# Attention values of two heads in one bank, with denominators from ScalarE's sums

## The chip, the cores and the metric

One NeuronCore of a Trainium2 chip runs the whole kernel. The metric is the device time in microseconds of one execution. Times inside the kernel come from one profiled execution, counted from the start of its span.

## The reference, cut to what matters

Two layers (DEPTH = 2) of a bidirectional encoder over 512 positions of width 1024, in float32. Each layer projects its normalised input, runs three mixers side by side (a Hyena convolution on 256 channels, grouped-query attention with 8 query heads and 2 key/value heads of 64, and multi-head latent attention, MLA, with 4 heads of 96 for scores and 64 for values), normalises each mixer's output, projects back, and then runs a gated feed-forward block of width 2816. The change is inside the two attentions:

```
s = einsum('bkgqd,bskd->bkgqs', qi, k) * scale
p = softmax(s, axis=-1)
o = einsum('bkgqs,bskd->bkgqd', p, v)
```

and the same for the four MLA heads, with a latent query and key of 64 + 32 and values of 64.

## The kernel before, in words

Every engine has its own program, in an order written out by hand, and the engines meet only at named semaphores. There is no planner: what stands behind a waiting instruction on its engine waits with it.

Activations are kept transposed (channels on partitions, the 512 positions along the free dimension). In the attention stage the twelve heads of a layer (h = 0 to 7 grouped-query, GH = 8; h = 8 to 11 MLA) pass one after another through a software pipeline. For a head TensorE does this:

- `scores(h)`: for each of four query chunks qc a bank 0 to 3 gets 128 queries by 512 keys. A grouped-query head uses two fp32r matmuls per chunk, on the rounded query with its low half (`q2`) below it; an MLA head one fp32 matmul, which runs as two passes. Chunk qc overwrites a bank that the exponentials of the head before must have read (`p_ready`), and grouped-query scores wait for `q2hi` and `q2lo` of their head.
- `turn(h, (0, 1))` and `turn(h, (2, 3))`: sixteen 128x128 transposes of the probabilities into banks 4 (even key chunk sc) and 5 (odd). A chunk waits until the one before it in the bank is copied out.
- `values(h)`: four fp32 matmuls (eight passes) into bank 6. The stationary tile has 128 columns: 64 of values and 64 of ones (the ones stand in `vg` and `mv`, set by two memsets of VectorE, lines 1438 and 1541). So 64 partitions of the bank get the output and the other 64 the denominator, repeated.
- `bank7(k)`: a piece of the MLA projections, two pieces per head for the first eight heads, in the order of the list `B7`: for each MLA head a query piece (6 passes), a rotation piece (a permutation, 2 passes) and a key piece (3 passes), then four value pieces. Bank 7 must be emptied by VectorE (`b7_free`) before the next one.
- `group(g)`: the sum of squares of a mixer's output.

TensorE's order (line 1161 on) is scores(h+1), the first bank-7 piece, turn(h, (0, 1)), values(h-1), turn(h, (2, 3)), the second bank-7 piece.

VectorE finds the maxima of a head's scores (`maxima`, which write `nm` and, scaled, `ns`), copies the odd turned chunks (`pt_copy`), does its part of the bank-7 pieces (for a rotation two products and a sum) and multiplies the output by the inverse denominator (`head_out`, line 1576). Its order is maxima(h+1), pt_copy(h, 1), bank-7 piece, head_out(h-1), pt_copy(h, 3), bank-7 piece.

ScalarE takes the exponentials (`exps`, four of 128x512), copies the even turned chunks, rounds the queries of head h+2 (`q_hi`, line 583) and forms the inverse denominators as Exp(-Ln(d)) on 64 partitions (`denominators`, line 714). Its order is pt_copy(h, 0), exps(h+1), q_hi(h+2), denominators(h-1), pt_copy(h, 2). The normalisation of the mixers (`group_squares`, `group_root`, `group_hi`) is put in at the last heads. GpSimd makes the low half of the rounded queries (`q_lo`, line 428).

Of the kernel before, what the change touches and what calls it, by code (L numbers as in the profile page):

```python
# [39 lines left out]
P = 128  # L40
DM, T, DEPTH = 1024, 512, 2
DC = DM // P
TC = T // P
# [62 lines left out]
def build(nc, a, out):  # L106
    ctx = ExitStack()
    with ctx:
# [29 lines left out]
        nm = sb("nm", [P, 2, TC])  # L138
        ns = sb("ns", [P, 2, TC])


# [83 lines left out]
        for name in (  # L225

                "ident_in", "fconst_in", "fw2_in", "const_in", "x_in0", "x_in1", "x_in2", "x_in3", "par_in", "w3_in",
                "filt_in", "tab_in", "mla_in", "raw0", "raw1", "out_sem",

                "raw_ok", "const_ok", "x_tr", "x_first", "fst_tr", "par_tr", "par_ok", "f_mm", "f_arg", "f_sin",  # L230

                "hi_ready", "lo_ready", "pe_item",

                "x_new", "gh_ready", "gl_ready", "xsq", "xsq_used", "xstat", "rbc_ready",

                "ysq", "ysq_used", "ycopy", "stat_post", "rms_post", "t_ready",

                "evac", "conv1", "conv_done", "nsq", "nstat", "nstd", "nrm", "nperm", "roped", "vtr", "vcopy", "khi", "klo",

                "fc_mm", "fc_done", "fd_mm", "fd_copy", "fd_done",  # L240

                "ha_mm", "hu_copy", "he_mm", "ho_mm", "he_copy", "h_prod", "hc_mm", "h_done",

                "q2hi", "q2lo", "s_tile", "nmax", "p_ready", "pt_tile", "pt_act", "pt_dve", "pv", "head_inv", "y_head",

                "mhi", "mlo", "kr_copy", "b7_full", "b7_free",

                "gsq", "gsq_used", "gstat", "gstd", "y_norm", "ygh", "ygl",

                "f_evac", "f_conv1", "f_conv", "f_gelu", "f_prod", "f_hi", "f_lo",  # L250

                "o_tr", "o_copy", "dve_self", "act_self"):
            S[name] = sem(name)
# [22 lines left out]
        assert len(B7) == 2 * GH  # L276
        HEADS = GH + MH


# [179 lines left out]
        def _(act):  # L459
# [83 lines left out]
            for lay in range(DEPTH):  # L543
# [127 lines left out]
                def group_root(g):  # L671

                    act.wait_ge(S["gstat"], lay * 3 + g + 1)

                    act.wait_ge(S["head_inv"], lay * HEADS + (GH, GH + 1, HEADS)[g])
# [20 lines left out]
                def exps(h):  # L696
                    scale = GD ** -0.5 if h < GH else MD ** -0.5
                    act.wait_ge(S["nmax"], lay * HEADS + h + 1)
                    if h >= 2:

                        act.wait_ge(S["pt_tile"], lay * 4 * HEADS + 4 * (h - 1))
                    for qc in range(TC):
                        A(prob[:, h % 2, qc, :], ps[:, qc, :], ACT.Exp, bias=ns[:, h % 2, qc:qc + 1],  # L703
                          scale=scale).then_inc(S["p_ready"], 1)

                def pt_copy(h, sc):

                    act.wait_ge(S["pt_tile"], lay * 4 * HEADS + 4 * h + sc + 1)
                    if h >= 2 and sc == 0:

                        act.wait_ge(S["pv"], lay * HEADS + h - 1)
                    A(probT[h % 2][:, sc, :], ps[:, 4, :], ACT.Copy).then_inc(S["pt_act"], 1)

                def denominators(h):

                    act.wait_ge(S["pv"], lay * HEADS + h + 1)
                    swapped = (h // 4) % 2 if h < GH else h % 2
                    o_rows = slice(GD, 2 * GD) if swapped else slice(0, GD)
                    d_rows = slice(0, GD) if swapped else slice(GD, 2 * GD)

                    if h >= 2:
                        act.wait_ge(S["y_head"], lay * HEADS + h - 1)
                    inverse_root(rr[o_rows, h % 2, :], std[o_rows, :], ps[d_rows, 6, :], 1,
                                 bias=False).then_inc(S["head_inv"], 1)

                exps(0)
                for h in range(HEADS):
                    pt_copy(h, 0)
                    if h + 1 < HEADS:
                        exps(h + 1)  # L730
                    if h + 2 < GH:
                        q_hi(h + 2)
                    if h:
                        denominators(h - 1)
                    pt_copy(h, 2)
                    if h == 1:
                        kr_copies()
                    if h == GH - 1:
                        group_squares(0)
                    if h == GH:  # L740
                        group_root(0)
                        act.wait_ge(S["y_head"], lay * HEADS + GH)
                        group_squares(1)
                    if h == GH + 1:
                        group_root(1)
                    if h == GH + 2:
                        group_hi(0)
                    if h == GH + 3:
                        group_hi(1)
                denominators(HEADS - 1)  # L750
                act.wait_ge(S["y_head"], lay * HEADS + HEADS)
                group_squares(2)
# [63 lines left out]
        def _(pe):  # L816
# [87 lines left out]
            for lay in range(DEPTH):  # L904
# [224 lines left out]
                def turn(h, tiles_):  # L1129

                    pe.wait_ge(S["p_ready"], (lay * HEADS + h) * 4 + 4)
                    for sc in tiles_:
                        if sc >= 2 or h:

                            k = (lay * HEADS + h) * 2 + sc // 2
                            pe.wait_ge(S["pt_act" if sc % 2 == 0 else "pt_dve"], k)
                        for qc in range(TC):
# [4 lines left out]
                def values(h):  # L1142

                    if h:
                        pe.wait_ge(S["y_head"], lay * HEADS + h)
                    if h == 0:
                        pe.wait_ge(S["vcopy"], lay + 1)
                    if h == GH:
                        pe.wait_ge(S["b7_free"], lay * len(B7) + len(B7))
                    pe.wait_ge(S["pt_act"], (lay * HEADS + h) * 2 + 2)  # L1150
                    pe.wait_ge(S["pt_dve"], (lay * HEADS + h) * 2 + 2)
                    for sc in range(TC):
                        if h < GH:
                            v = vg[:, sc, (h // 4) * GD:(h // 4) * GD + P]
                        else:
                            i = h - GH
                            v = mv[:, sc, i // 2, (i % 2) * MV:(i % 2) * MV + P]
# [17 lines left out]
                values(HEADS - 1)  # L1175

# [15 lines left out]

                pe.wait_ge(S["y_head"], lay * HEADS + HEADS)
                pe.wait_ge(S["gstd"], lay * 3 + 3)
# [48 lines left out]
        def _(dve):  # L1243
# [60 lines left out]
            for lay in range(DEPTH):  # L1304
# [235 lines left out]

                V.do(nc.vector.memset(mv[:, :, :, MV:2 * MV], 1.0))
                def maxima(h):
# [7 lines left out]
                def pt_copy(h, sc):  # L1550

                    dve.wait_ge(S["pt_tile"], (lay * HEADS + h) * 4 + sc + 1)
                    if h >= 2 and sc == 1:

                        dve.wait_ge(S["pv"], lay * HEADS + h - 1)
                    copy(probT[h % 2][:, sc, :], ps[:, 5, :]).then_inc(S["pt_dve"], 1)
# [18 lines left out]

                def head_out(h):

                    swapped = (h // 4) % 2 if h < GH else h % 2
                    o_rows = slice(GD, 2 * GD) if swapped else slice(0, GD)
                    rows = slice((h % 2) * GD, (h % 2 + 1) * GD)  # L1580
                    dst = qf[rows, h // 2, :] if h < GH else cq[rows, (h - GH) // 2, :]
                    if h < GH:

                        dve.wait_ge(S["q2lo"], lay * GH + h + 1)
                    dve.wait_ge(S["head_inv"], lay * HEADS + h + 1)
                    tt(dst, ps[o_rows, 6, :], rr[o_rows, h % 2, :], ALU.mult).then_inc(S["y_head"], 1)

# [4 lines left out]
                for h in range(HEADS):  # L1592
# [5 lines left out]
                    if h == GH + 3:  # L1598
                        dve.wait_ge(S["y_head"], lay * HEADS + GH)
                        group_norm(1)  # L1600
                    if h:
                        head_out(h - 1)
                    pt_copy(h, 3)
# [8 lines left out]
                    if h == GH + 3:  # L1612
                        group_lo(0)
                        group_lo(1)
                head_out(HEADS - 1)
                dve.wait_ge(S["y_head"], lay * HEADS + HEADS)
                group_sum(2)
# [141 lines left out]
```

## Time and profile before

| | us |
|---|---|
| median of 3 runs | 1548.88 (1548.32 to 1549.81) |
| profiled execution, its own time | 1550.24 |
| its span in the profile | 1548.2 |
| TensorE matmuls busy | 1428.5 (92%) |
| VectorE busy | 923.2 (60%) |
| ScalarE busy | 612.1 (40%) |
| GpSimd busy | 521.2 (34%) |

The profile calls the engines PE (TensorE matmuls), PEld (its weight loads), DVE (VectorE), ACT (ScalarE) and POOL (GpSimd). L1158 is line 1158 of the kernel. A matmul's end is modelled, so how long a matmul occupies the engine is read from the start of the next one. A granted clock of 1.00 is 2.4 GHz, half of it 1.2 GHz. "[2.08 <-POOL q L433]" behind an instruction says that its engine sat idle for 2.08 us before it and that GpSimd's instruction of line 433 ended this. The attention stage of layer 0 lies between about 205 and 330 us, that of layer 1 between about 963 and 1088 us.

### The profile page before, as it was taken

To read this page: it belongs to the slowest core of one execution; us is meant where nothing else is said; L and a number is where in the kernel's file an instruction comes from. 1 tells how busy PE (TensorE), PEld (TensorE's weight loads), DVE (VectorE), ACT (ScalarE), POOL (GpSimd) and SP (SyncE) were. 2 spreads that over 40 slices of the span, in tenths; PEclk is the share of its full clock that TensorE was granted. 3 is DMA by queue.
4 is the path that set the end of the run, shared out by engine and by line. 5 is a ranking of instruction groups with operands and counts; after the bars stand their busy time and mean duration, and the time that the engine had idled before them with its cause. 6 is when DMAs were issued, how large, how long until landed. Compare 5 with 4: busy or idle time off the path is not lost.

```text
span 1548.2 us, 14920 instructions
## 1 busy us (share of the span) xinstructions
PE 1428.5 (92%) x5759; PEld 1056.5 (68%) x5759; DVE 923.2 (60%) x1033; ACT 612.1 (40%) x867; POOL 521.2 (34%) x243
## 2 busy tenths in 40 slices
PE   5898989988899999999978898999979999999997
PEld 3576746556688888878755775664757888887885
DVE  5636777564678787711166567666465878785112
ACT  5222255653444444332241224556344444433222
POOL 2312211014444444444441213100354444444444
PEclk8999999999899999999989999999989999999998
DMA  7211100002133333323241112000112333332231
GB/s 241 74 28 54 48 28 1 1 28 82 41 96 95 95 96 95 92 85 97 80 136 41 55 31 72 1 1 1 55 55 82 96 96 95 95 95 89 86 102 64
DMA packets 195167, 108.52 MB, mean 70 GB/s; under 512 B 5895, under 2 KB 193657, under 8 KB 194202
## 3 DMA queue, kind: packets, MB, share of 16 engines
q1 hardware_dynamic: 195098, 107.58, 23.5%
q8 instruction: 46, 0.75, 0.2%
q14 instruction: 23, 0.19, 0.0%
HBM read 105.47 MB, written 2.10 MB: 69 GB/s over the span
## 4 chain that ended last, share of the span: by engine, by line
PE 75%; DVE 11%; ACT 6%; issue 3%; POOL 3%; DMA 1%; POOLq 0%; SPq 0%; DVEq 0%; ACTq 0%
PE ps L877 19%; PE ps L879 19%; PE ps L878 19%; PE ps L1158 3%; PE ps L984 2%; PE ps L945 2%; DVE nm L1546 2%; PE ps L971 2%; ACT prob L703 2%; POOL xT L416 2%; POOL wl L409 1%; PE ps L887 1%; ACT rr L479 1%; PE ps L1138 1%; ACT wh L468 1%
## 5 line engine op out<-in xcount | busy, mean ns | idle before, releaser
L409 POOL TENSOR_TENSOR wl<-raw,wh 128x1024 fp32r<-128x1024 f32 x184 | 443.5, 2412 | 895.6 <-ACT wh L468 895.6
L468 ACT ACTIVATE wh<-raw 128x1024 fp32r<-128x1024 f32 x184 | 194.9, 1060 | 613.4 <-PE ps L879 608.7
L877 PE MATMUL ps<-gh,wh 128*128 128x512 f32 (+1 forms) x896 | 365.2, 408 | 11.2 <-POOL wl L409 11.2
L879 PE MATMUL ps<-gh,wl 128*128 128x512 f32 (+1 forms) x896 | 355.7, 397 | 0.0
L878 PE MATMUL ps<-gl,wh 128*128 128x512 f32 (+1 forms) x896 | 355.5, 397 | 0.0
L877 PEld LDWEIGHTS ps<-gh,wh 128*128 128x128 f32 (+1 forms) x896 | 167.6, 187 | 58.6 <-issue 12.6
L878 PEld LDWEIGHTS ps<-gl,wh 128*128 128x128 f32 (+1 forms) x896 | 167.7, 187 | 45.8 <-issue 4.7
L879 PEld LDWEIGHTS ps<-gh,wl 128*128 128x128 f32 (+1 forms) x896 | 167.7, 187 | 42.8
L1651 DVE SCALAR_TENSOR_TENSOR cv<-pad,pm,cv 128x512 f32<-128x512 f32 x88 | 130.6, 1484 | 84.0 <-ACT cv L779 84.0
L1260 DVE TENSOR_TENSOR acc<-acc,sq 128x512 f32<-128x512 f32 x24 | 60.6, 2523 | 195.9 <-ACT sq L508 195.7
L877 PE MATMUL ps<-fh,wh 128*128 128x512 f32 x352 | 139.3, 396 | 3.2 <-POOL wl L409 3.2
L878 PE MATMUL ps<-fl,wh 128*128 128x512 f32 x352 | 139.0, 395 | 0.0
L879 PE MATMUL ps<-fh,wl 128*128 128x512 f32 x352 | 139.0, 395 | 0.0
L1638 DVE TENSOR_TENSOR fl<-fprod,fh 128x512 fp32r<-128x512 f32 x44 | 103.9, 2362 | 15.2 <-ACT fh L792 15.2
L877 PEld LDWEIGHTS ps<-fh,wh 128*128 128x128 f32 x352 | 66.0, 187 | 20.2 <-ACT wh L468 4.0
L879 PEld LDWEIGHTS ps<-fh,wl 128*128 128x128 f32 x352 | 66.0, 187 | 16.2
L878 PEld LDWEIGHTS ps<-fl,wh 128*128 128x128 f32 x352 | 66.0, 187 | 16.0
L779 ACT ACTIVATE cv<-pad,pm 128x512 f32<-128x512 f32 x88 | 70.5, 803 | 0.0
L1654 DVE SCALAR_TENSOR_TENSOR cv<-pad,pm,cv 128x512 f32<-128x512 f32 x88 | 66.2, 752 | 3.1
L1646 DVE TENSOR_TENSOR pad<-ps,rbc 128x512 f32<-128x512 f32 x88 | 56.4, 684 | 18.9 <-ACT rbc L479 18.9
L703 ACT ACTIVATE prob<-ps,ns 128x512 f32<-128x512 f32 x96 | 58.1, 690 | 18.3 <-DVE ns L1548 18.1
L1138 PEld LDWEIGHTS ps<-ident,prob 128*128 128x128 f32 x384 | 44.5, 141 | 25.1 <-issue 19.8
(224 smaller groups left out, 1950.2 us busy)
## 6 DMA issues: line engine op xcount, KB each, us to landing
raw<-w_up SPq DMA_DIRECT2D x88, 512.0 KB, 3.8
raw<-w_down SPq DMA_DIRECT2D x32, 512.0 KB, 3.6
raw<-w_in SPq DMA_DIRECT2D x30, 512.0 KB, 3.9
raw<-w_out SPq DMA_DIRECT2D x16, 512.0 KB, 3.6
raw<-w_down SPq DMA_DIRECT2D x16, 384.0 KB, 3.2
xio<-x SPq DMA_DIRECT2D x4, 512.0 KB, 5.7
win<-c_win SPq DMA_DIRECT2D x2, 1024.0 KB, 5.5
TF<-c_tf SPq DMA_DIRECT2D x2, 1024.0 KB, 10.0
```

The lines of the kernel that those rows point to most:

```text
L409: nc.gpsimd.tensor_tensor(wl[:, slot, :], raw[:, slot, :], wh[:, slot, :].bitcast(F32), ALU.subtract).then_inc(S["lo_ready"], 1)
L468: A(wh[:, slot, :], raw[:, slot, :], ACT.Copy).then_inc(S["hi_ready"], 1)
L703: A(prob[:, h % 2, qc, :], ps[:, qc, :], ACT.Exp, bias=ns[:, h % 2, qc:qc + 1], scale=scale).then_inc(S["p_ready"], 1)
L779: A(cv[:, k, :], pad[:, k, 1:T + 1], ACT.Identity, scale=pm[:, bass.ds(col + j + (PM["ffn_w1"] + k * FC), 1)], bias=pm[:, bass.ds(col + j ...
L877: mm(ps[0:cols, bank, :], w_hi, x_hi, start=start and k == 0, stop=False)
L878: mm(ps[0:cols, bank, :], w_hi, x_lo, start=False, stop=False)
L879: ins = mm(ps[0:cols, bank, :], w_lo, x_hi, start=False, stop=stop and k == tile_n - 1)
L1138: ins = nc.tensor.transpose(ps[:, 4 + sc % 2, qc * P:(qc + 1) * P], prob[:, h % 2, qc, sc * P:(sc + 1) * P], ident[:])
L1260: tt(acc[:], acc[:], sq[:, m % 2, :], ALU.add).then_inc(S["ysq_used"], 1)
L1638: tt(fl[:, j:j + 1, :], fprod[:].rearrange("p (o t) -> p o t", o=1), fh[:, j:j + 1, :].bitcast(F32), ALU.subtract).then_inc(S["f_lo"], 1)
L1651: V.do(stt(out=c, in0=pad[:, k, 0:T], scalar=pm[:, bass.ds(col + j + (PM["ffn_w0"] + k * FC), 1)], in1=c, op0=ALU.mult, op1=ALU.add))
L1654: stt(out=c, in0=pad[:, k, 2:T + 2], scalar=pm[:, bass.ds(col + j + (PM["ffn_w2"] + k * FC), 1)], in1=c, op0=ALU.mult, op1=ALU.add).then_i ...
```

## The change

Heads are taken in six pairs (PAIRS = HEADS // 2).

- `values(p)` of TensorE now does both heads of a pair: for each of four key chunks, one matmul of 64 value columns for the even head into partitions 0 to 63 of bank 6 and one for the odd head into partitions 64 to 127. The ones and their memsets are gone.
- It no longer stands between the two turn pairs of each head. It stands, with a new `inverses(p)`, before the first turns of each even head from 2 on, and at the end.
- The exponentials also sum their row (`accum_out`) into `den`. VectorE takes the reciprocal for a pair (`denominators(p)`, in odd heads), ScalarE spreads it over 64 columns per head (`inv_wide`, into `std`), TensorE turns that in four transposes into bank 4 (`inverses`), and ScalarE copies it to `rr` (`inv_copy`).
- ScalarE's Ln and Exp of the denominators are gone. The output is multiplied once per pair on 128 partitions (`pair_out`).
- The exponentials of head h (from 2 on) wait for the reciprocal of the pair before; the turns of an even head wait for `inv_copy`.
- The roots and high halves of mixer groups 0 and 1 on ScalarE move by up to one head, and wait for `inv_tile`, since they share `std`.

```diff
 exps(h), ScalarE
+                    if h >= 2:
+                        act.wait_ge(S["den_inv"], lay * PAIRS + h // 2)
...
                         A(prob[:, h % 2, qc, :], ps[:, qc, :], ACT.Exp, bias=ns[:, h % 2, qc:qc + 1],
-                          scale=scale).then_inc(S["p_ready"], 1)
+                          scale=scale, accum_out=den[:, h % 2, qc:qc + 1]).then_inc(S["p_ready"], 1)
...
+                def inv_wide(p):
+                    act.wait_ge(S["den_inv"], lay * PAIRS + p + 1)
+                    if p:
+                        act.wait_ge(S["inv_tile"], lay * PAIRS + p)
+                    A(std[:].rearrange("p (c h d) -> p h c d", c=TC, h=2), inv[:].unsqueeze(3).to_broadcast([P, 2, TC, GD]),
+                      ACT.Copy).then_inc(S["inv_wide"], 1)
+                def inv_copy(p):
+                    act.wait_ge(S["inv_tile"], lay * PAIRS + p + 1)
+                    if p >= 2:
+                        act.wait_ge(S["y_pair"], lay * PAIRS + p - 1)
+                    A(rr[:, p % 2, :], ps[:, 4, :], ACT.Copy).then_inc(S["inv_copy"], 1)
                 exps(0)
                 for h in range(HEADS):
+                    if h and h % 2 == 0:
+                        inv_copy(h // 2 - 1)
                     pt_copy(h, 0)
                     if h + 1 < HEADS:
                         exps(h + 1)
                     if h + 2 < GH:
                         q_hi(h + 2)
-                    if h:
-                        denominators(h - 1)
                     pt_copy(h, 2)
+                    if h % 2:
+                        inv_wide(h // 2)
...
 TensorE
+                def inverses(p):
+                    pe.wait_ge(S["inv_wide"], lay * PAIRS + p + 1)
+                    pe.wait_ge(S["pt_act"], (lay * HEADS + 2 * p + 1) * 2 + 2)
+                    for qc in range(TC):
+                        at = slice(qc * P, (qc + 1) * P)
+                        ins = nc.tensor.transpose(ps[:, 4, at], std[:, at], ident[:])
+                    ins.then_inc(S["inv_tile"], 1)
...
                     for sc in range(TC):
-                        if h < GH:
-                            v = vg[:, sc, (h // 4) * GD:(h // 4) * GD + P]
...
-                        ins = mm(ps[:, 6, :], v, probT[h % 2][:, sc, :], start=(sc == 0), stop=(sc == TC - 1))
+                        for half in range(2):
+                            if p < GH // 2:
+                                at = 2 * GD * (p // 2)
+                                v = vg[:, sc, at:at + GD]
+                            else:
+                                v = mv[:, sc, p - GH // 2, 2 * MV * half:2 * MV * half + MV]
+                            ins = mm(ps[half * GD:(half + 1) * GD, 6, :], v, probT[half][:, sc, :], start=(sc == 0), stop=(sc == TC - 1))
...
                         bank7(2 * h)
+                    if h and h % 2 == 0:
+                        inverses(h // 2 - 1)
+                        values(h // 2 - 1)
                     turn(h, (0, 1))
-                    if h:
-                        values(h - 1)
                     turn(h, (2, 3))
...
 VectorE
-                V.do(nc.vector.memset(vg[:, :, GD:2 * GD], 1.0))
-                V.do(nc.vector.memset(mv[:, :, :, MV:2 * MV], 1.0))
+                def denominators(p):
+                    dve.wait_ge(S["p_ready"], (lay * HEADS + 2 * p + 1) * 4 + 4)
+                    if p:
+                        dve.wait_ge(S["inv_wide"], lay * PAIRS + p)
+                    nc.vector.reciprocal(inv[:], den[:]).then_inc(S["den_inv"], 1)
+                def pair_out(p):
+                    dst = qf[:, p, :] if p < GH // 2 else cq[:, p - GH // 2, :]
...
+                    tt(dst, ps[:, 6, :], rr[:, p % 2, :], ALU.mult).then_inc(S["y_pair"], 1)
...
-                    if h:
-                        head_out(h - 1)
+                    if h % 2:
+                        denominators(h // 2)
+                    elif h:
+                        pair_out(h // 2 - 1)
                     pt_copy(h, 3)
```

## Rows read from the trace of the kernel before

**Rows 1.** The page, part 4: the chain of work that ended last, by engine

```profile
PE 75%; DVE 11%; ACT 6%; issue 3%; POOL 3%; DMA 1%; POOLq 0%; SPq 0%; DVEq 0%; ACTq 0%
```

**Rows 2.** Stretches: length, busy (xcount) PE, PEld, DVE, ACT, POOL; clock, DMA

```profile
224.46:290.50 66.04, 64.62 (x271) 40.01 (x269) 42.63 (x79) 39.81 (x67) 6.38 (x5) 1.00 0.00 1
290.50:327.40 36.90, 33.23 (x126) 17.93 (x124) 24.87 (x43) 24.97 (x42) 0.00 (x0) 1.00 0.00 1
991.58:1057.60 66.02, 64.60 (x264) 39.11 (x263) 42.52 (x80) 39.69 (x67) 5.10 (x4) 1.00 0.00 0
```

**Rows 3.** Timeline of head 1: start, length, engine, line, what [idle before <-releaser]

```profile
224.46 1.04 PE L1138 MATMUL ps<-ident,prob 128*128 128x128 f32 x8
...
225.10 0.60 ACT L712 ACTIVATE probT<-ps 128x512 f32<-128x512 f32 x1 [5.88 <-PE ps L1138]
...
225.34 3.60 PE L1158 MATMUL ps<-probT,vg 128*128 128x512 f32 x8
225.54 0.69 DVE L1556 COPY probT<-ps 128x512 f32<-128x512 f32 x1 [0.89 <-PE ps L1138]
225.59 2.42 ACT L703 ACTIVATE prob<-ps,ns 128x512 f32<-128x512 f32 x4
...
228.03 0.63 ACT L588 ACTIVATE q<-qf 64x512 fp32r<-64x512 f32 x1
...
228.81 1.27 POOL L433 TENSOR_TENSOR q<-qf,q 64x512 fp32r<-64x512 f32 x1 [8.66 <-ACT q L588]
...
229.56 0.47 PE L1116 MATMUL ps<-cqh,uqh 128*96 128x512 f32 x1
...
231.03 0.39 PE L1093 MATMUL ps<-ka,q 128*128 128x512 f32 x1
...
232.84 1.02 PE L1119 MATMUL ps<-mqf,perm_m 96*96 96x512 f32 x2
...
233.71 1.04 PE L1138 MATMUL ps<-ident,prob 128*128 128x128 f32 x8
```

**Rows 4.** Groups of 225 to 290: line, engine, shapes, xcount | busy, mean ns

```profile
L1122 PE MATMUL ps<-ckl,ukh 128*64 128x512 f32 x3 | 1.2, 394 | 0.0
```

**Rows 5.** Timeline of head 0

```profile
214.70 1.03 PE L1138 MATMUL ps<-ident,prob 128*128 128x128 f32 x8
...
216.07 1.10 PE L1138 MATMUL ps<-ident,prob 128*128 128x128 f32 x8 [0.34 <-ACT probT L712]
...
217.11 1.10 PE L1119 MATMUL ps<-mqf,perm_m 96*96 96x512 f32 x2
...
220.29 0.47 PE L1093 MATMUL ps<-ka,q 128*128 128x512 f32 x1 [2.08 <-POOL q L433]
...
223.51 0.63 PE L1122 MATMUL ps<-ckh,ukh 128*64 128x512 f32 x1
```

**Rows 6.** Timeline of head 5, VectorE: its copy and its part of the rotation

```profile
263.77 0.69 DVE L1556 COPY probT<-ps 128x512 f32<-128x512 f32 x1
...
265.69 0.69 DVE L1568 TENSOR_TENSOR mqf<-yt 96x512 f32<-96x512 f32 x1
```

**Rows 7.** Chain of waits, window of layer 0's attention: start, length, what

```profile
270.64 0.69 PE ps L1126 x3
...
277.21 3.44 PE ps L1100 x8
```

**Rows 8.** Timeline of the last four heads

```profile
306.57 3.60 PE L1100 MATMUL ps<-mkf,mqf 96*128 96x512 f32 x8
...
324.29 3.67 PE L1158 MATMUL ps<-probT,mv 128*128 128x512 f32 x8 [1.88 <-DVE probT L1556]
```

**Rows 9.** Timeline ahead of head 0

```profile
205.80 0.48 DVE L1541 MEMSET mv<- 128x512 f32 x1 [0.17 <-DVE ckv L1397]
```

**Rows 10.** Groups of the whole span, ScalarE

```profile
L533 ACT ACTIVATE pm<-ps 128x88 f32<-128x88 f32 (+1 forms) x6 | 1.2, 240 | 3.3 <-PE ps L847 3.3
```

More of the change, by code:

```diff
@@ L139, in build @@
         ns = sb("ns", [P, 2, TC])
+        den = sb("den", [P, 2, TC])
+        inv = sb("inv", [P, 2, TC])
         with ExitStack() as s:
@@ L277, in build @@
         HEADS = GH + MH
+        PAIRS = HEADS // 2
         @block.sync
@@ L709, in pt_copy @@
                     if h >= 2 and sc == 0:
-                        act.wait_ge(S["pv"], lay * HEADS + h - 1)
+                        act.wait_ge(S["pv"], lay * PAIRS + h // 2)
                     A(probT[h % 2][:, sc, :], ps[:, 4, :], ACT.Copy).then_inc(S["pt_act"], 1)
[L714 to L724, printed above, removed]
+                def inv_wide(p):
[9 more added lines that the diff above has]
+                    A(rr[:, p % 2, :], ps[:, 4, :], ACT.Copy).then_inc(S["inv_copy"], 1)
                 exps(0)
                 for h in range(HEADS):
+                    if h and h % 2 == 0:
+                        inv_copy(h // 2 - 1)
                     pt_copy(h, 0)
@@ L740, in _ @@
                     if h == GH:
+                        act.wait_ge(S["inv_tile"], lay * PAIRS + GH // 2)
                         group_root(0)
-                        act.wait_ge(S["y_head"], lay * HEADS + GH)
+                        act.wait_ge(S["y_pair"], lay * PAIRS + GH // 2)
                         group_squares(1)
-                    if h == GH + 1:
+                    if h == GH + 2:
+                        act.wait_ge(S["inv_tile"], lay * PAIRS + GH // 2 + 1)
                         group_root(1)
-                    if h == GH + 2:
                         group_hi(0)
@@ L749, in _ @@
                         group_hi(1)
-                denominators(HEADS - 1)
-                act.wait_ge(S["y_head"], lay * HEADS + HEADS)
+                inv_copy(PAIRS - 1)
+                act.wait_ge(S["y_pair"], lay * PAIRS + PAIRS)
                 group_squares(2)
@@ L1136, in turn @@
                             pe.wait_ge(S["pt_act" if sc % 2 == 0 else "pt_dve"], k)
+                        if h and h % 2 == 0 and sc == 0:
+                            pe.wait_ge(S["inv_copy"], lay * PAIRS + h // 2)
                         for qc in range(TC):
@@ L1174, in _ @@
                         group(h - GH)
-                values(HEADS - 1)
+                inverses(PAIRS - 1)
+                values(PAIRS - 1)
                 def gate_out(k):
@@ L1191, in _ @@
                     tiles(lay, I_OUT + m, m, m, DC, yh, yl, 0, True, True, gate=gate_out, ks=range(ready, DC))
-                pe.wait_ge(S["y_head"], lay * HEADS + HEADS)
+                pe.wait_ge(S["y_pair"], lay * PAIRS + PAIRS)
                 pe.wait_ge(S["gstd"], lay * 3 + 3)
@@ L1553, in pt_copy @@
                     if h >= 2 and sc == 1:
-                        dve.wait_ge(S["pv"], lay * HEADS + h - 1)
+                        dve.wait_ge(S["pv"], lay * PAIRS + h // 2)
                     copy(probT[h % 2][:, sc, :], ps[:, 5, :]).then_inc(S["pt_dve"], 1)
@@ L1574, in bank7 @@
                         copy(mv[:, i, :, 2 * MV:3 * MV], v[:, :, 1, MN:MN + MV]).then_inc(S["b7_free"], 1)
[L1576 to L1586, printed above, removed]
+                def denominators(p):
+                    dve.wait_ge(S["p_ready"], (lay * HEADS + 2 * p + 1) * 4 + 4)
+                    if p:
+                        dve.wait_ge(S["inv_wide"], lay * PAIRS + p)
+                    nc.vector.reciprocal(inv[:], den[:]).then_inc(S["den_inv"], 1)
+                def pair_out(p):
+                    dst = qf[:, p, :] if p < GH // 2 else cq[:, p - GH // 2, :]
+                    if p < GH // 2:
+                        dve.wait_ge(S["q2lo"], lay * GH + 2 * p + 2)
+                    dve.wait_ge(S["pv"], lay * PAIRS + p + 1)
+                    dve.wait_ge(S["inv_copy"], lay * PAIRS + p + 1)
+                    tt(dst, ps[:, 6, :], rr[:, p % 2, :], ALU.mult).then_inc(S["y_pair"], 1)
                 maxima(0)
@@ L1614, in _ @@
                         group_lo(1)
-                head_out(HEADS - 1)
-                dve.wait_ge(S["y_head"], lay * HEADS + HEADS)
+                pair_out(PAIRS - 1)
+                dve.wait_ge(S["y_pair"], lay * PAIRS + PAIRS)
                 group_sum(2)
```

21 lines of the change are left out of this document (8 added, 13 removed).

## The prediction

> **What bounds the kernel now.** I read three views. The chain that ended last gives TensorE 75% of the span [rows 1]. The stretches show what its attention stage is like: from head 1's first turn to head 8's it takes 66.04 us with TensorE busy for 64.62 at full clock, and layer 1 repeats it to 0.02 us; the last four heads, to the end of the last values, take 36.90 us with 33.23 busy [rows 2]. So the stage is TensorE's, with almost nothing left over in the first part. The timeline of one head shows why [rows 3]: after the turns of score chunks 0 and 1 begin (224.46) a chain runs elsewhere. ScalarE copies chunk 0 at 225.10, takes head 2's four exponentials from 225.59, and rounds head 3's queries at 228.03; GpSimd makes their low half from 228.81 to 230.08. Only then may TensorE start head 3's scores. It never notices: values(0) stand in that place from 225.34, eight passes of 0.43 us, 3.43 in all, then two more turns and a piece for bank 7 (229.56), and the scores start at 231.03, 0.95 us after they could. The change touches just this place.
>
> **What the change does to the work.** Below, a is the start of a head's turns of chunks 0 and 1, and V the time of one pair's values.
>
> *Values.* Before: 8 passes a head. After: 16 passes for two heads, each of 64 stationary columns. A pass of 64 columns streams the same 512 and costs the same (394 ns modelled, as the 96-column ones around it) [rows 4], so there is no gain unless the two halves of the array work at once. Bounds: 16 passes in a row, 6.86 us a pair as now; all of them in twos, 3.43 us. I take V = 4.3, ten pass times. No row shows two halves in use, so this is a judgement: the diff alternates the halves after every matmul, and they share no stationary column, no moving tile and no output partition. The turn for both ends goes into the range.
> The Trainium skill, "TensorE: Matmul & The Clock Gate", Part 3 (packing small matmuls), says that matmuls whose outputs start in different column groups run concurrently, and gives 2.38 times for three tiles; at that efficiency (0.79 of ideal) an estimate for two is 6.86/1.59 = 4.3 us. Against the change, "TensorEngine Tiling (Array Packing)", Key Properties, says that changing the tiling mode drains the array, and each pair now does so twice. No row here shows either.
>
> *Inverses.* Four turns of 128 columns a pair: the eight of head 1 take 0.88 us (224.46 to 225.34), so 0.44, 12 times. They need ScalarE's wide copy, which lies behind the second copy of the odd head and ends at about a + 7, ahead of the next scores' end (below): no wait. ScalarE's copy back (0.6) fits into V. The reciprocal (VectorE, 128x8) costs at most what the smallest row there costs, some 0.2.
>
> *The move.* This is the expensive part. values() leaves its place between a head's two turn pairs and goes ahead of the first, for even heads only. Now the two turn pairs follow each other, and the chain ScalarE copy, exponentials, query copy, GpSimd, next scores has only 2.4 us of turns and one bank-7 piece over it. How long the chain is can be read where no values stand in between even now, at head 0 [rows 5]: turns at 214.70, second turns 216.07 (they wait for the copy out of bank 4), next piece 217.11, and head 2's scores at 220.29 after 2.08 us idle for GpSimd. That is a + 5.59. It holds for every head 0 to 5 afterwards. In head 1 the same sum gives 230.08 + 0.15 - 224.46 = 5.77; I use 5.6.
>
> *The new wait.* Exponentials of an even head overwrite den, so they wait for the reciprocal, which VectorE takes in the odd head before only after its copy of chunk 1 (ends a + 1.77) and a bank-7 piece. A copy of 0.68 makes that a + 2.5 instead of a + 1.13: +1.4 us on the chain in heads 1 and 3. In head 5 the piece is the rotation, which ends 2.61 us after the copy begins [rows 6], so at a + 3.7, and exponentials at a + 3.9: +2.8. Queued behind it on ScalarE are the query copy and the second copy; behind these GpSimd and the scores.
>
> *The walk.* Scores 1.81 (231.03 to 232.84), rotation piece 0.87, query piece 1.47, key or value piece 0.69, MLA scores 3.43 [rows 3, 7]. Time from one head's turns to the next one's:
> head 1: 5.6 + 1.4 + 1.81 + 0.87 + 0.44 + V = 10.12 + V
> head 2: 5.6 + 1.81 + 1.47 = 8.88
> head 3: 5.6 + 1.4 + 1.81 + 0.69 + 0.44 + V = 9.94 + V
> head 4: 5.6 + 1.81 + 0.87 = 8.28
> head 5: 5.6 + 2.8 + 1.81 + 0.69 + 0.44 + V = 11.34 + V
> Heads 6 and 7 feed MLA scores, which need no query copy and wait only for the first exponential: 3.2 + 3.43 + 0.69 = 7.32 and 3.2 + 3.43 + 0.44 + V = 7.07 + V.
> Sum 62.95 + 4V; with V = 4.3 it is 80.1 against 66.04: +14.1 us a layer, although the passes themselves got 10 us shorter.
> Last four heads: after head 8's turns ScalarE does copy, exponentials, copy (a + 4.3), root (1.35), four squares; VectorE's sums end at a + 9.1, its maxima of head 10 at 11.75, copy and reciprocal at 12.65, so head 11's scores start at 13.85 (now 306.57 - 290.50 = 16.07 [rows 8]). Then 3.43 + 0.44 + V to head 10's turns, and from there 10.2 (exponentials, root and the high halves on ScalarE, the norm and reciprocal on VectorE, wide copy, inverses) + V to the end: 27.9 + 2V = 36.5 against 36.90, -0.4.
>
> *Clock.* In head 0 TensorE passed from full to half clock in that 2.08 us gap, in both layers: the scores behind it took 220.29 to 223.51, 3.22 us instead of 1.81, with 0.2 more in the piece after [rows 5]. An idle of 1.88 us at 324.29 left the clock up [rows 8]. The gaps of the walk run from the end of the bank-7 piece (which starts at 2.5 when VectorE has emptied the bank, 3.95 where it rotates first) to the next scores: 7.0 - 3.97 = 3.0, 7.0 - 3.4 = 3.6 and 8.4 - 4.65 = 3.7 us in heads 1, 3 and 5, 5.6 - 4.65 = 0.9 and 5.6 - 3.97 = 1.6 in heads 2 and 4. I count three falls of 1.6 us a layer: +4.8 (bounds 0 and 5 x 1.6 = 8).
>
> *Rest.* The memset of mv lay ahead of the first maxima [rows 9]: -0.4. Sums beside the exponentials: no row has such an operation. Bounds: nothing, and one small ScalarE instruction each, 0.24 us [rows 10]. I take 0.1 each, 4 on the chain in some 6 heads: +2.4 (0 to 5.8). Ln and Exp of the denominators (1.22 us a head) leave ScalarE, and VectorE multiplies 128 partitions once for two heads: neither was late, so nothing. What follows the last values (norm of group 2) has 8 us of output passes over it, as before.
>
> *Sum.* A layer: 14.1 - 0.4 + 4.8 + 2.4 - 0.4 = +20.5; two: +41. The profiled execution took 1550.24 us (span 1548.2), so 1591.2; the median of the runs is 1.4 lower: **1590 us**.
>
> **The rivals.**
> *The halves do not overlap.* V = 6.86: the walk gives 90.4 (+24.4) and the last four 41.6 (+4.7), with the other terms +35.9 a layer, +72: 1621. For it: every pass in the trace starts 0.43 us after the one before, whatever its columns. Against it: none of these passes went to another part of the array.
> *TensorE stays the bound.* If the chain were covered, each layer would save 6 x (6.86 - 4.3) - 6 x 0.44 = 12.7 us, two 25: 1523, faster. Its place is the start of scores(h+2). It decides from where the chain ends before a + 3.4 to 4.0, when turns and bank-7 piece are done; it would have to be 2 us shorter than head 0 shows it. For it only TensorE's 98% busy; against it the order of the instructions.
> *No difference.* The overlap's gain (15.4 a layer) and a chain seen in part only just cancel: 1549. This needs half of the stalls to be absent; nothing speaks for it.
> *The clock stays down.* If all of heads 1 to 7 ran at half clock, scores (5 x 1.81 + 2 x 3.43), pieces (about 6) and values (17) would take as long again: +39 a layer in place of 4.8, 1658. For it: TensorE would be busy for some 70% of that stretch; against it: after head 0 the clock was up again at the end of one head's scores.
>
> **How the numbers follow.** Forecast 0.58, no overlap 0.27, TensorE the bound 0.07, no difference 0.03, clock down 0.05. Within the forecast the ends are 1565 (V = 3.43, no fall of the clock, free sums) and about 1610; no overlap reaches to 1628 with dear sums. The range 1568 to 1628 leaves out the fast cases, the clock and little else. A measurement of this kernel tells 0.2%, 3 us, from no change. Slower by more: 0.90; within: 0.03; faster: 0.07.
>
> **What would show it.** Scores of heads 2 to 7 preceded by idle time of TensorE, ended by GpSimd, of 3 us or more behind odd heads and 1 to 1.6 behind even ones; turn pairs back to back with 0.5 us for the copy; exponentials of even heads starting after the reciprocal; granted clock under 1 in the stretch of heads 1 to 7; 16 passes of values in some 4.3 us (starts under 0.43 apart) or in 6.9. Wrong, if these scores start without a wait, if that stretch is under 66 us, or if the wait is ended by something other than GpSimd's low half.

## The result

The changed kernel takes 1604.7 us (median, 1601.82 to 1605.62) against 1549.35 us for the kernel before on the same chip (median of 1548.32, 1548.88, 1549.81 and one stray execution of 3313.44 us, which the interval leaves out); ratio 1.036, 95% interval 1.034 to 1.038. The forecast was 1590 us in a range of 1568 to 1628. Way and cause were right. Two terms, the clock and the last four heads, were too small, and V was too large, so that the errors partly cancelled.

The page after gives TensorE slightly more busy time, and its chain of waits more TensorE, ScalarE and GpSimd than [rows 1]:

```profile
PE 1432.1 (90%) x5807; PEld 1055.9 (66%) x5807; DVE 921.4 (58%) x1029; ACT 602.5 (38%) x939; POOL 521.3 (33%) x243
```
```profile
PE 77%; DVE 9%; ACT 7%; POOL 4%; issue 4%; DMA 1%; POOLq 0%; SPq 0%; DVEq 0%; ACTq 0%
PE ps L892 18%; PE ps L890 18%; PE ps L891 18%; PE ps L1184 3%; ACT prob L708 3%; PE ps L997 2%; PE ps L958 2%; PE ps L984 2%; PE ps L1106 2%; PE ps L1154 2%; POOL xT L419 1%; PE ps L1113 1%; PE ps L1107 1%; POOL wl L412 1%; PE ps L900 1%
```

Busy time is a little longer although the passes of values now overlap, because passes at the lower clock take longer. The line that has grown most is the first half of the grouped-query scores: 64 instructions, behind 43.2 us of idle time, 35.4 of them ended by GpSimd's low half of the queries.

```profile
L1106 PE MATMUL ps<-ka,q 128*128 128x512 f32 x64 | 39.1, 612 | 43.2 <-POOL q L436 35.4
```

Stretches of layer 0 from head 1's first turns to head 8's, and from there to the first output pass (columns as in [rows 2]: length, busy time of PE, PEld, DVE, ACT, POOL, granted clock, DMA):

```profile
224.35:314.75 90.40, 70.24 (x294) 41.69 (x292) 44.92 (x84) 38.10 (x89) 6.30 (x5) 0.85 0.00 1
314.75:355.68 40.93, 31.80 (x127) 16.86 (x125) 22.29 (x38) 22.63 (x50) 0.00 (x0) 0.79 0.00 1
```

66.04 us have become 90.40, 36.90 have become 40.93, and the granted clock is 0.85 and 0.79 where it was 1.00 [rows 2]. In layer 1 the same two stretches take 89.45 and 38.55 us at clock 0.87:

```profile
1009.55:1099.00 89.45, 69.30 (x294) 40.95 (x292) 44.71 (x84) 38.09 (x89) 6.30 (x5) 0.87 0.00 0
1099.00:1137.55 38.55, 29.41 (x127) 15.65 (x125) 22.43 (x38) 22.58 (x50) 0.00 (x0) 0.87 0.00 1
```

Before they took 66.01 (982.34 to 1048.35) and 36.89 (to 1085.24). Together that is 28.4 us more in layer 0 and 25.1 in layer 1, 53.5 in all; the profiled spans differ by 51.8 (1600.0 against 1548.2), so the rest of the kernel is 1.7 us shorter.

Head 1 in the timeline answers to [rows 3]; there the scores of head 3 began 6.57 us after the turns (224.46 to 231.03) with values inside, here 7.54 after, with none:

```profile
224.35 1.03 PE L1154 MATMUL ps<-ident,prob 128*128 128x128 f32 x8
...
224.99 0.60 ACT L717 ACTIVATE probT<-ps 128x512 f32<-128x512 f32 x1 [5.89 <-PE ps L1154]
...
225.73 1.10 PE L1154 MATMUL ps<-ident,prob 128*128 128x128 f32 x8 [0.34 <-ACT probT L717]
...
226.63 0.18 DVE L1607 RECIPROCAL inv<-den 128x8 f32<-128x8 f32 x1
...
226.90 0.69 ACT L708 ACTIVATE prob<-ps,ns 128x512 f32<-128x512 f32 x1 [1.31 <-PE ps L1154]
...
227.49 0.19 ACT L708 ACTIVATION_READ_ACCUMULATOR prob<-ps,ns 128x1 f32 x1
...
227.58 0.68 ACT L708 ACTIVATE prob<-ps,ns 128x512 f32<-128x512 f32 x1
...
229.71 0.63 ACT L591 ACTIVATE q<-qf 64x512 fp32r<-64x512 f32 x1
...
230.48 1.26 POOL L436 TENSOR_TENSOR q<-qf,q 64x512 fp32r<-64x512 f32 x1 [10.47 <-ACT q L591]
230.98 0.63 ACT L725 ACTIVATE std<-inv 128x512 f32<-128x512 f32 x1
...
231.89 0.77 PE L1106 MATMUL ps<-ka,q 128*128 128x512 f32 x1 [3.50 <-POOL q L436]
...
235.44 1.91 PE L1132 MATMUL ps<-mqf,perm_m 96*96 96x512 f32 x2
...
237.14 0.75 PE L1164 MATMUL ps<-ident,std 128*128 128x128 f32 x4
...
237.82 3.65 PE L1184 MATMUL ps<-probT,vg 128*64 128x512 f32 x16
...
241.41 0.77 PE L1154 MATMUL ps<-ident,prob 128*128 128x128 f32 x5
```

The reader sees: the second turns at a + 1.38, after the copy; the reciprocal at 226.63 and the exponentials right behind it (226.90); the sum's read (0.19) behind each, so that four exponentials take 2.8 us instead of 2.4; the query copy at 229.71, GpSimd at 230.48, the scores at 231.89. Scores and rotation then last 5.25 us at half clock (to 237.14) where they took 2.68 before. And the 16 passes of values take 3.59 us (237.82 to 241.41). The scores of heads 4 to 7 wait in the same way:

```profile
247.56 0.66 PE L1106 MATMUL ps<-ka,q 128*128 128x512 f32 x1 [1.46 <-POOL q L436]
...
260.09 0.77 PE L1106 MATMUL ps<-ka,q 128*128 128x512 f32 x1 [4.15 <-POOL q L436]
...
274.98 0.76 PE L1106 MATMUL ps<-ka,q 128*128 128x512 f32 x1 [1.91 <-POOL q L436]
...
288.20 0.77 PE L1106 MATMUL ps<-ka,q 128*128 128x512 f32 x1 [4.22 <-POOL q L436]
```

Two more gaps of 1.26 us lie ahead of the bank-7 pieces that wait for VectorE's rotation (245.20 and 283.08).

### The profile page after: what moved, and what is told of

Read it like the earlier page. It is cut to its first block, busy times and chain, and to the rows that moved or that the text cites. A ratio compares the mean times of both kernels' runs of the same rounds, so it can differ in the third digit from the quotient of the medians.

```text
span 1600.0 us, 15092 instructions
## 1 busy us (share of the span) xinstructions
PE 1432.1 (90%) x5807; PEld 1055.9 (66%) x5807; DVE 921.4 (58%) x1029; ACT 602.5 (38%) x939; POOL 521.3 (33%) x243
## 4 chain that ended last, share of the span: by engine, by line
PE 77%; DVE 9%; ACT 7%; POOL 4%; issue 4%; DMA 1%; POOLq 0%; SPq 0%; DVEq 0%; ACTq 0%
PE ps L892 18%; PE ps L890 18%; PE ps L891 18%; PE ps L1184 3%; ACT prob L708 3%; PE ps L997 2%; PE ps L958 2%; PE ps L984 2%; PE ps L1106 2%; PE ps L1154 2%; POOL xT L419 1%; PE ps L1113 1%; PE ps L1107 1%; POOL wl L412 1%; PE ps L900 1%
## 5 line engine op out<-in xcount | busy, mean ns | idle before, releaser
L1684 DVE SCALAR_TENSOR_TENSOR cv<-pad,pm,cv 128x512 f32<-128x512 f32 x88 | 130.7, 1485 | 83.5 <-ACT cv L792 83.5
L1572 DVE TENSOR_REDUCE nm<-ps 128x1 f32<-128x512 f32 x96 | 63.8, 688 | 47.0 <-PE ps L1107 38.0
L1106 PE MATMUL ps<-ka,q 128*128 128x512 f32 x64 | 39.1, 612 | 43.2 <-POOL q L436 35.4
L1154 PE MATMUL ps<-ident,prob 128*128 128x128 f32 x384 | 55.7, 290 | 22.0 <-ACT probT L717 16.2
L708 ACT ACTIVATE prob<-ps,ns 128x512 f32<-128x512 f32 x96 | 64.6, 689 | 24.9 <-DVE ns L1574 11.8
```

The lines of the kernel that those rows point to most:

```text
L1106: mm(ps[:, qc, :], q2[:, h % 2, cols], ka[:, h // 4, :], start=True, stop=False)
L1572: V.do(nc.vector.reduce_max(nm[:, h % 2, qc:qc + 1], ps[:, qc, :], AX.X))
L1684: V.do(stt(out=c, in0=pad[:, k, 0:T], scalar=pm[:, bass.ds(col + j + (PM["ffn_w0"] + k * FC), 1)], in1=c, op0=ALU.mult, op1=ALU.add))
```

## The experiments

All times are medians, each beside runs of the kernel before on the same chip (1548.8 to 1549.1 us in these); ratios are to it, with a 95% interval. The changed kernel was timed once, apart from these, so a difference to its 1604.7 us leans on the kernel before having agreed within 0.6 us each time; and each timeline is one execution, the changed kernel's being the fastest of its four (1601.82). The stretch rows are of layer 0, from head 1's first turns to head 8's, and have the columns above.

**The place alone.** The kernel before with one move:

```diff
+                    if h:
+                        values(h - 1)
                     turn(h, (0, 1))
-                    if h:
-                        values(h - 1)
                     turn(h, (2, 3))
```

> The kernel before with one thing moved: TensorE's values(h-1) stand ahead of a head's first turns instead of between its two turn pairs; ones columns, Ln and Exp and all waits stay. Theory (the loss is the place): every grouped-query head now shows the chain of copy, exponentials, query copy, GpSimd (a + 5.6 to the next scores), so heads 1 to 7 take some 80 us instead of 66 a layer at full clock and about 90 with the clock falling in the gaps; 1590 to 1605 us, GpSimd ending the waits of the scores. Rival (the loss is in what was added: inverse turns, sums, copies, the reciprocal's wait): within 5 us of 1549.

Measured 1604.6 us, ratio 1.037 (1.035 to 1.038). Its stretches, and one of its scores:

```profile
227.42:310.17 82.75, 69.85 (x271) 40.64 (x269) 44.37 (x81) 39.53 (x67) 6.31 (x5) 0.98 0.00 0
310.17:354.73 44.56, 34.61 (x117) 17.97 (x116) 23.77 (x40) 24.95 (x42) 0.00 (x0) 0.89 0.00 1
```
```profile
257.64 0.69 PE L1093 MATMUL ps<-ka,q 128*128 128x512 f32 x1 [2.23 <-POOL q L433]
```

82.75 us instead of 66.04, and 44.56 instead of 36.90: moving values and nothing else costs as much as the whole change. The gaps in front of the scores are 1.1 to 2.2 us, ended by GpSimd. That the totals agree is partly chance, for the loss is spread otherwise: here values move in every head and keep their 3.43 us, the first stretch grows by 16.7 us and not 24.4, 3.0 us come ahead of it (values(0) now stand before head 1's turns), and of the 7.7 us in the last four heads most is another wait, values behind VectorE's copy (3.97 us idle at 338.44, 3.27 at 349.99). At 0.98 its clock stays up better than in the changed kernel, so the stretch has little of the clock's part. The rival is out.

**The query copy first.** Changed kernel, ScalarE:

```diff
                 for h in range(HEADS):
+                    if h + 2 < GH:
+                        q_hi(h + 2)
                     if h and h % 2 == 0:
                         inv_copy(h // 2 - 1)
                     pt_copy(h, 0)
                     if h + 1 < HEADS:
                         exps(h + 1)
-                    if h + 2 < GH:
-                        q_hi(h + 2)
```

> The changed kernel with q_hi(h+2) put first in ScalarE's iteration instead of behind the exponentials. Theory: GpSimd's low half is then made long before the scores need it, these wait only for the exponentials of their bank, TensorE's gaps fall from 3.5 to 4.2 us to under 1.5 and the clock mostly stays up; heads 1 to 7 shrink from 90 to some 67 us, the kernel to about 1557 us. Rival (the exponentials and the reciprocal's wait are the long part, the query copy only the last link): 1590 or more, with ScalarE ending the same gaps.

Measured 1549.8 us, ratio 1.0017 (1.0006 to 1.0027): 55 us back from one moved line, 7 more than the theory expected.

```profile
220.15:287.14 66.99, 61.56 (x295) 34.69 (x293) 45.19 (x86) 36.70 (x88) 5.44 (x5) 1.00 0.00 1
```

66.99 us at full clock. So the gaps and the falls of the clock behind them go together; this run does not price the two apart. In its timeline the exponentials of head 2 start at 223.32 and head 3's scores at 224.65, 1.3 us behind, with no wait for GpSimd:

```profile
223.32 0.69 ACT L708 ACTIVATE prob<-ps,ns 128x512 f32<-128x512 f32 x1 [1.94 <-PE ps L1154]
...
224.65 0.40 PE L1106 MATMUL ps<-ka,q 128*128 128x512 f32 x1
```

**The reciprocal first.** Changed kernel, VectorE: `denominators(h // 2)` ahead of `maxima(h + 1)` in odd heads instead of behind `bank7(2 * h)`.

> The changed kernel with the reciprocal first in VectorE's iteration of the odd heads instead of behind its copy and the bank-7 piece. Theory: exponentials of even heads start some 1.1 us earlier after heads 1 and 3 and 2.5 after head 5; 4.7 us a layer, so 1593 to 1596 us, less if a fall of the clock goes with it. Rival (that wait is hidden behind something else): 1604.

Measured 1582.4 us, ratio 1.022 (1.021 to 1.024), twice the expected gain:

```profile
223.13:302.40 79.27, 64.89 (x295) 38.42 (x293) 45.36 (x83) 37.63 (x89) 6.29 (x5) 0.94 0.00 1
```

79.27 us instead of 90.40. The gaps behind heads 1, 3 and 5 are 2.06, 2.59 and 1.46 us instead of 3.50, 4.15 and 4.22: that accounts for 5.8 of the 11. The rest came with the clock, 0.94 instead of 0.85. It does not follow the gap's length: the scores behind gaps of 2.06 and 1.91 us ran at full clock here, those behind 1.44 and 1.46 us mostly at half.

**The halves one after the other.** Changed kernel, in `values(p)`:

```diff
-                    for sc in range(TC):
-                        for half in range(2):
+                    for half in range(2):
+                        for sc in range(TC):
```

> The changed kernel with the two halves of values(p) one after the other (all four key chunks of the even head, then of the odd one) instead of in turns; same 16 passes. Theory (the two halves of the array work at once when neighbours in the order differ in their half): values take some 6.7 us instead of 3.6, on the path for each pair, 12 x 3.1 = 37 us: about 1640. Rival (a pass of 64 columns is cheap by itself, or the overlap is only in the modelled ends): 1604.

Measured 1617.9 us, ratio 1.046 (1.044 to 1.047): slower than the changed kernel, by 13 us and not 36. The weight loads of one values group tell why. In the changed kernel (start, length, count in one burst) every 0.43 us brings two:

```profile
265.86 0.14 PEld L1184 LDWEIGHTS ps<-probT,vg 128*64 128x64 f32 x2 [0.29 <-issue]
266.29 0.14 PEld L1184 LDWEIGHTS ps<-probT,vg 128*64 128x64 f32 x2 [0.29 <-issue]
```

In this one they come singly, then in the middle two and three at a time, then singly again:

```profile
264.59 0.14 PEld L1184 LDWEIGHTS ps<-probT,vg 128*64 128x64 f32 x1 [0.29 <-issue]
...
265.44 0.19 PEld L1184 LDWEIGHTS ps<-probT,vg 128*64 128x64 f32 x3 [0.29 <-issue]
265.87 0.19 PEld L1184 LDWEIGHTS ps<-probT,vg 128*64 128x64 f32 x2 [0.24 <-issue]
...
267.22 0.14 PEld L1184 LDWEIGHTS ps<-probT,vg 128*64 128x64 f32 x1 [0.29 <-issue]
```

So the halves do work at once: the group takes 5.35 us (263.68 to 269.03), 12.5 pass times, and not 6.9. Taken strictly in order, only the last pass of one half and the first of the other could overlap, 15 pass times or 6.4 us; so the engine seems to take the second half's passes while several of the first are still to run. Each of 12 groups is 1.76 us longer, 21 us in all, and 8 of them come back with the clock (0.91 instead of 0.85):

```profile
223.26:316.82 93.56, 73.44 (x295) 41.74 (x293) 44.44 (x84) 38.06 (x89) 6.30 (x5) 0.91 0.00 1
```

Why it stays up better is not shown. Head 1 makes it plain: up to there the two kernels run the same instructions, and the gap is the same, yet scores and rotation piece take 2.78 us (230.79 to 233.57) at full clock here and 5.25 at half in the changed kernel.

```profile
230.79 0.47 PE L1106 MATMUL ps<-ka,q 128*128 128x512 f32 x1 [3.49 <-POOL q L436]
...
232.71 1.02 PE L1132 MATMUL ps<-mqf,perm_m 96*96 96x512 f32 x2
233.57 0.60 PE L1164 MATMUL ps<-ident,std 128*128 128x128 f32 x4
```

**The clock held up.** Changed kernel, with matmuls for nothing in the gaps ahead of the scores of heads 3 to 7:

```diff
+                def warm(g):
+                    if g // 2:
+                        pe.wait_ge(S["y_pair"], lay * PAIRS + g // 2)
+                    n = 12 if g % 2 else 5
+                    for i in range(n):
+                        mm(ps[:, 6, :], ka[:, 0, 0:P], ka[:, 1, :], start=(i == 0), stop=(i == n - 1))
...
                 def scores(h):
+                    if 3 <= h < GH:
+                        warm(h - 2)
```

> The changed kernel with idle time of TensorE filled: ahead of the scores of heads 3 to 7 it runs 12 (behind odd heads) or 5 (behind even heads) rounded matmuls into the free bank 6, whose results nothing uses. Theory (the falls of the clock are a term of their own, some 10 us a layer beside the waits): the scores and pieces behind the gaps run at full clock, granted clock of heads 1 to 7 near 1.00 instead of 0.85, and the kernel gains 15 to 20 us although TensorE does more: about 1587. Rival (the walk's waits make all of the loss and a low clock only fills what would be waiting): 1604 or more.

Measured 1584.7 us, ratio 1.023 (1.022 to 1.025): 20 us less by doing more.

```profile
224.35:305.02 80.67, 70.97 (x341) 43.68 (x339) 43.52 (x84) 38.10 (x89) 6.35 (x5) 1.00 0.00 1
```
```profile
231.89 0.47 PE L1115 MATMUL ps<-ka,q 128*128 128x512 f32 x1 [0.78 <-POOL q L436]
...
233.79 1.02 PE L1141 MATMUL ps<-mqf,perm_m 96*96 96x512 f32 x2
234.65 0.60 PE L1173 MATMUL ps<-ident,std 128*128 128x128 f32 x4
```

The scores of head 3 start at the same 231.89, but scores and rotation take 2.76 us (to 234.65) instead of 5.25. The stretch is 80.67 us at clock 1.00. The scores still wait for GpSimd behind each filled gap (0.31 to 1.48 us), so the filling held nothing up. The walk gives 62.95 + 4 x 3.59 = 77.3 with V as measured, plus 0.36 in each of heads 1 to 5 for the sums, 79.1. So the 90.40 of that execution are 80.7 of waits and work and 9.7 of clock.

**Without the sums.** Changed kernel, exponentials without `accum_out`, `den` set to ones.

> The changed kernel without the sums beside the exponentials; den is set to ones once a layer, so the outputs are not normalised. Theory (a read of the sum behind each exponential, 0.09 us more from one to the next, stands on the chain to the next scores, 0.36 us a head in heads 1 to 5, 9 and 10): about 6 us less, 1598. Rival (ScalarE has room, the sums are free): 1604. Second rival (shorter gaps let the clock stay up behind even heads): 1590 or less.

Measured 1594.3 us, ratio 1.029 (1.028 to 1.031): 10 us less, between the theory (6) and its second rival (15). Its four executions lie at 1591.8, 1591.9, 1596.6 and 1597.6 us; the profiled one is the third.

```profile
222.97:310.28 87.31, 68.98 (x295) 40.61 (x293) 44.60 (x84) 35.54 (x61) 6.32 (x5) 0.88 0.00 1
```

The stretch is 3.1 us shorter. The five gaps ahead of scores are 0.35 to 0.38 us shorter each (3.12, 1.08, 3.79, 1.55 and 3.87 us), and so are two in the last four heads (0.84 and 1.71 instead of 1.20 and 2.06): 2.5 us a layer, 5 in all, is the reads. The rest goes with the clock, 0.88 instead of 0.85.

**Both first.** Changed kernel with both moves.

> The changed kernel with both the query copy first on ScalarE and the reciprocal first on VectorE. Theory: behind odd heads the scores now wait for the exponentials alone, and these start 1.1 to 2.5 us earlier; with the query copy early 2 to 3 us a layer are left to gain from that, so 1544 to 1546 us, against 1549.8 with the query copy alone. Rival (with the query copy early, TensorE is the bound of those heads too): 1549.8.

Measured 1544.6 us, ratio 0.997 (0.996 to 0.998), as expected:

```profile
221.81:286.89 65.08, 59.38 (x294) 35.47 (x293) 44.54 (x85) 36.62 (x88) 5.46 (x5) 1.00 0.00 1
```

**Values split over the turns.** Both moves, a new order on TensorE, and in even heads VectorE empties bank 7 before its copy. The copies of chunks 0 and 1 wait for the first part (a semaphore of its own), those of 2 and 3 for the second.

```diff
-                    if h < GH:
+                    if h < GH and h % 2 == 0:
                         bank7(2 * h)
                     if h and h % 2 == 0:
                         inverses(h // 2 - 1)
-                        values(h // 2 - 1)
+                        values(h // 2 - 1, (0, 1))
                     turn(h, (0, 1))
+                    if h < GH and h % 2:
+                        bank7(2 * h)
+                    if h and h % 2 == 0:
+                        values(h // 2 - 1, (2, 3))
                     turn(h, (2, 3))
...
                 inverses(PAIRS - 1)
-                values(PAIRS - 1)
+                values(PAIRS - 1, (0, 1))
+                values(PAIRS - 1, (2, 3))
```

> Both moves and a new order on TensorE: a pair's values in two parts, key chunks 0 and 1 ahead of the even head's first turns and 2 and 3 between its turn pairs; in odd heads the first bank-7 piece stands between the turn pairs; VectorE empties bank 7 ahead of its copy in even heads. Theory (nothing but order kept the gain of the overlapping halves away): TensorE is the bound again in heads 1 to 7, whose work is some 54 us a layer against 66.04 before, the last four heads stay near 40: 1525 to 1532 us, faster than both. Rival (ScalarE and VectorE are the bound as soon as values are short): 1542 or more.

Measured 1531.6 us, ratio 0.988 (0.986 to 0.990), faster than both kernels:

```profile
219.25:280.02 60.77, 57.56 (x289) 35.12 (x287) 46.60 (x87) 36.63 (x88) 6.65 (x5) 1.00 0.00 1
280.02:318.20 38.18, 31.61 (x135) 15.80 (x133) 22.63 (x40) 22.63 (x50) 0.00 (x0) 0.87 0.00 1
```

TensorE is busy for 57.56 of 60.77 us: it is nearly the bound again, 5.3 us a layer ahead of [rows 2], though not at the 54 hoped for. Three orders change at once here, so what each gives is not shown.

**And the last four heads.** In these the changed kernel waits for VectorE's copy, which stands behind the maxima, and they behind the sum of group 1 (327.21), and for ScalarE's copy, behind root and high halves (343.57):

```profile
327.21 1.12 PE L1154 MATMUL ps<-ident,prob 128*128 128x128 f32 x4 [2.92 <-DVE probT L1582]
```
```profile
343.57 1.94 PE L1154 MATMUL ps<-ident,prob 128*128 128x128 f32 x8 [2.06 <-ACT probT L717]
```

So the squares and the sum of group 1 go to head 9, its statistic to head 10 (between the turns), ScalarE's high halves of group 0 to head 11.

> The kernel with split values, and in the last four heads the squares and the sum of mixer group 1 moved from head 8 to head 9 (ScalarE, VectorE), its statistic on TensorE to head 10, and both high-half passes of ScalarE to head 11. Theory (the 40 us of the last four heads come from VectorE's maxima standing behind that sum and ScalarE's copies standing behind squares and high halves, and from the low clock in the gaps this opens): gaps of 1.2, 2.9, 2.1 and 1.0 us there mostly go, the last four heads take 33 us or less instead of 40, 1515 to 1522 us. Rival (the exponentials and maxima of heads 9 to 11 bound that part by themselves): 1528 or more.

Measured 1518.2 us, ratio 0.980 (0.978 to 0.982):

```profile
218.20:278.97 60.77, 57.55 (x290) 35.13 (x288) 46.58 (x87) 36.64 (x88) 6.67 (x5) 1.00 0.00 1
278.97:310.24 31.27, 27.15 (x135) 14.13 (x133) 22.68 (x40) 22.52 (x50) 0.00 (x0) 1.00 0.00 1
```

31.27 us instead of 38.18 in the kernel it builds on and 36.90 before; the clock stays at 1.00. This is the fastest version, 31 us below the kernel before, and it keeps every part of the change: halves side by side, sums, reciprocal, inverse turns.

## Why the prediction was right, and what it mis-sized

*The chain takes the place of values.* Right. The place alone costs 56 us, and the query copy ahead of the exponentials gives 55 back. The walk gave the periods well at full clock: 79.1 against 80.67 measured with the clock held; 0.4 of the rest is that the four inverse turns take 0.53 us (264.85 to 265.38) and not 0.44. The gaps came where it put them, 3.50, 4.15 and 4.22 us for 3.0, 3.6 and 3.7, and 1.46 and 1.91 for 0.9 and 1.6.

*V = 4.3.* The halves overlap, so the first rival (1621) did not come; V is 3.59, 8.4 pass times, closer to the lower bound. Over 12 groups this made the forecast 8.5 us too high. The estimate worked out from the Trainium skill, "TensorE: Matmul & The Clock Gate", Part 3 (2.38 times for three tiles), was too cautious: here it is 6.86/3.59 = 1.91 times for two. The trace agrees with that page's statement that such matmuls run concurrently. The drain that the Trainium skill, "TensorEngine Tiling (Array Packing)", Key Properties, names for a change of mode can be only a few tenths of a microsecond here: 0.15 us in the group (3.59 - 8 x 0.43), 0.09 in the inverse turns ahead of it, and 0.14 in the eight turns behind it in the run with split values (230.09 to 231.11, against 0.88).

*Clock, +4.8 a layer.* This term failed. The clock fell behind even heads too, and a fall costs up to 2.5 us and not 1.6: 5.25 us for scores and rotation instead of 2.76. The held clock puts it at 9.7 us in the first stretch of layer 0, and the last four heads ran at 0.79 there and at 0.87 in layer 1, where the walk had counted no fall. I had taken head 0 as the price, where the clock came back in time for the next piece; in the changed kernel it stays at 0.50 from 231.89 to 237.14. And the fall in head 0 came just behind the gap, not in it: the first pass took 0.30 us, the next 0.36, then 0.43. No rule by the gap's length would have given the number: the same 3.5 us behind head 1 left the clock at half in the changed kernel and at full with the halves one after the other.

*Last four heads, -0.4.* Measured +4.0 in layer 0 and +1.7 in layer 1. The walk at full clock puts head 10's turns at 17.7 + 3.59 = 21.3 after head 8's; they came at 24.2 (338.97 - 314.75), with the scores of head 11 at half clock for their first part, and in layer 1 at 22.9. How much of the miss is the clock and how much are waits that the walk had too short is not separated; the last experiment shows that moving the work of group 1 and the high halves takes the waits and the low clock away together.

*The reciprocal's wait, +1.4, +1.4, +2.8.* The size of the wait was right (exponentials at a + 2.55 in head 1 against a + 1.13 [rows 3], 255.11 - 252.43 = 2.7 in head 3 and 283.22 - 279.34 = 3.9 in head 5). Undone it gave 22 us rather than the 11 of the waits (5.8 a layer measured), and the rest came with a higher clock.

*The sums, 0.1 each.* Right in size: exponentials follow each other at 0.66 to 0.68 us instead of 0.58, and seven gaps a layer are 0.35 to 0.38 us longer by them, 2.5 us for the +2.4 forecast.

*TensorE the bound.* This rival described what the change could give, not what it did: with the chain moved out of the way, the kernel reaches 1518.2, close to the 1523 worked out there (though other moves had to be added for it).

*The sum.* That the forecast came within 15 us owes something to luck: with V = 3.59 and every other term as forecast it would have been 1581.5, 23 us short and not 15, with some 10 of that from the clock of heads 1 to 7 and most of the rest from the last four heads. The range still held it.

*A row misread.* The third row of [rows 2] runs from head 2's turns to head 9's, not from head 1's to head 8's as the prediction has it. The right stretch of layer 1 is 66.01 us, so the reading that layer 1 repeats layer 0 stands.

Not settled: what decides whether the clock falls behind a gap. Layer 1 lost 3 us less than layer 0, 2.4 of them in the last four heads: behind the same gap of 2.06 us the eight turns of head 10 ran at half clock in layer 0 and at full in layer 1 (343.57, shown above, against this line):

```profile
1126.52 1.06 PE L1154 MATMUL ps<-ident,prob 128*128 128x128 f32 x8 [2.06 <-ACT probT L717]
```

## What to carry to other kernels

Before moving a block of TensorE work, ask what runs elsewhere under it: here 3.4 us of values hid a chain over ScalarE and GpSimd, and the move cost more than nearly halving that work gave. If the chain has to stay, start its slow link first; one line of order was worth 55 us. And price an exposed gap with the clock that falls in it: the gaps of heads 1 to 7, 1.3 to 4.2 us long and 17.8 in all, brought 9.7 us of low clock with them. Treat that price as wide: the falls did not follow the length of the gaps.

## What the runs showed of the hardware

Two matmuls of 64 stationary columns whose outputs lie in different halves of a bank's partitions run at the same time: 16 passes in 3.59 us against 6.86, which is twice the 3.43 of eight passes in a row. They need not be neighbours in the order: with eight passes of one half ahead of eight of the other the group takes 5.35 us, less than the 6.4 of a strict order. Filling gaps with matmuls for nothing made the kernel 20 us faster. Whether the clock falls behind a gap is not told by its length: scores ran mostly at half clock (0.57 granted) behind 1.44 us of idle time in one run, at full behind 3.49 us in another, and at half behind 3.50 us after the same instructions. A sum beside an exponential is a second instruction of 0.19 to 0.22 us on ScalarE, of which 0.09 shows.
